# Expert blocks of 96 rows of one expert and 32 of the same or of a guest expert, in place of whole and half blocks; shared expert added to the residual before the routed experts

## The reference, cut to what matters

```python
T, D_MODEL, N_EXPERTS, MOE_TOPK, EXPERT_FF = 512, 1024, 64, 8, 256

def swiglu(h, wg, wu, wd):
    return (jax.nn.silu(h @ wg) * (h @ wu)) @ wd

def moe_ffn(h, ...):
    ...                                  # top_e, gw: 8 experts of each token and their weights
    # the tokens of each expert are laid out in blocks of 128 rows, padded
    def step(y, blk):
        tok, wt, e = blk
        out = swiglu(hf[tok], exp_gate[e], exp_up[e], exp_down[e])
        return y.at[tok].add(out.astype(F32) * wt[:, None]), None
    y, _ = lax.scan(step, jnp.zeros((T, D), F32), ...)
    shared = swiglu(hf, sh_gate, sh_up, sh_down)
    return (y.astype(h.dtype) + shared).reshape(B, S, D)

x = x + g2 * moe_ffn(h2, ...)
x = rms_norm_2(x, final_g)
```

## Time and profile before

| | us |
|---|---|
| median of 3 runs (2342.84 to 2349.06) | 2344.48 |
| span of the profiled execution | 2343.3 |
| first gate/up product of the experts starts | 1681.69 |
| last down product ends (2261.55 + 3.65) | 2265.20 |
| blocks stored | 51 (17 trips of 3) |

### The profile page before, as it was taken

One profiled execution on the slowest core, in us unless ns is written; L12 is line 12 of the kernel. 1 busy time (PEld: TensorE's weight loads), 2 busy tenths in 40 slices (PEclk: granted clock), 3 DMA queues, 4 the chain that ended last, 5 costly groups with the idle time before them and its releaser, 6 DMA issues. The chain is left out here.

```text
span 2343.3 us, 27600 instructions
## 1 busy us (share of the span) xinstructions
PE 2151.4 (92%) x10395; PEld 1246.3 (53%) x10395; DVE 1330.6 (57%) x2524; ACT 461.2 (20%) x916; POOL 396.7 (17%) x771
## 2 busy tenths in 40 slices
PE   6999989999999999999879999998699999999975
PEld 3444554777785458883443788445333333333322
DVE  3448863766672134434968333535766766767745
ACT  2013561121120011004235232011011111111111
POOL 0005000111000000000000000000444444444433
PEclk9999999999999999999989999998799999999988
DMA  9422000535524015981111100401499999898976
GB/s 389 180 81 81 36 1 20 233 144 216 215 81 179 36 72 229 391 306 54 37 57 58 51 3 4 177 36 54 180 372 397 425 353 421 344 407 357 413 281 252
DMA packets 68999, 446.60 MB, mean 191 GB/s; under 512 B 12276, under 2 KB 12932, under 8 KB 44066
## 3 DMA queue, kind: packets, MB, share of 16 engines
q0 software_dynamic: 36176, 254.42, 27.1%
q1 hardware_dynamic: 32722, 190.78, 21.0%
HBM read 416.27 MB, written 73.45 MB: 209 GB/s over the span
## 5 line engine op out<-in xcount | busy, mean ns | idle before, releaser
L965 PE MATMUL psum<-arena 128*128 128x256 f32 x1904 | 416.7, 381 | 2.1 <-PEq L1005 2.0
L2824 PE MATMUL psum<-arena 128*64 128x512 f32 (+1 forms) x1088 | 366.1, 600 | 38.9 <-DVE arena L2872 16.6
L965 PEld LDWEIGHTS psum<-arena 128*128 128x128 f32 x1904 | 361.4, 190 | 62.6 <-issue 14.0
L2872 DVE STREAM_TRANSPOSE arena<-arena 32x256 f32<-32x256 f32 x832 | 362.1, 435 | 15.8 <-DMA arena<-scratch_h,arena 4.1
L2824 PEld LDWEIGHTS psum<-arena 128*64 128x64 f32 (+1 forms) x1088 | 143.8, 165 | 226.6 <-issue 197.7
L2815 PE MATMUL psum<-arena 128*64 128x512 f32 (+1 forms) x544 | 186.2, 598 | 1.2 <-ACT arena L2850 1.2
L1067 PE MATMUL psum<-arena 128*128 128x512 f32 x352 | 151.8, 592 | 0.3 <-PEq L1091 0.3
L2815 PEld LDWEIGHTS psum<-arena 128*64 128x64 f32 (+1 forms) x544 | 68.5, 163 | 113.2 <-issue 111.8
L869 PE MATMUL psum<-arena 128*128 128x512 f32 x256 | 111.2, 593 | 2.3 <-DVE arena L2432 1.5
L1067 PEld LDWEIGHTS psum<-arena 128*128 128x128 f32 x352 | 66.6, 190 | 83.4 <-issue 83.4
L2878 DVE COPY arena<-psum 128x512 f32<-128x512 f32 x51 | 35.3, 692 | 132.7 <-PE psum L2815 132.7
(11 more groups left out here) (521 smaller groups left out, 2932.0 us busy)
## 6 DMA issues: line engine op xcount, KB each, us to landing
scratch_expert_out<-arena SPq DMA_DIRECT2D x18, 2048.0 KB, 19.9
scratch_expert_out<-arena SPq DMA_DIRECT2D x51, 512.0 KB, 9.9
arena<-in_w_ada SPq DMA_DIRECT2D x12, 2048.0 KB, 16.8
arena<-in_ada_w POOLq DMA_DIRECT2D x12, 2048.0 KB, 8.8
arena<-in_w_up SPq DMA_DIRECT2D x22, 1024.0 KB, 4.8
arena<-in_w_in SPq DMA_DIRECT2D x9, 2048.0 KB, 11.0
arena<-in_w_down SPq DMA_DIRECT2D x5, 2048.0 KB, 8.6
arena<-in_w_o SPq DMA_DIRECT2D x2, 2048.0 KB, 8.4
```

Of the source, the lines that this page charges most:

```text
L965: last = pe.matmul(out, w[:, k, :], x[:, k, :], start=(k == 0), stop=(k == KH - 1))
L2824: last = pe.matmul(K.bank[2 + s][r, :], xt[:, s, P * k + r.start:P * k + r.stop], gu[:, lane, 2 * E_FF * k:2 * E_FF * (k + 1)], start=(k = ...
L2872: last = dve.transpose(channels[c:c + 32, :, a:a + 32], tokens[a:a + 32, :, c:c + 32])
```

## The change

Blocks of 128 rows stay, and so do three lanes a trip. Each block has now a host expert on rows 32 to 127 and, on rows 0 to 31, either the host again or a guest expert. A host's part of more than 96 tokens takes all 128 rows; experts of up to 32 tokens are one guest piece, experts of 33 to 64 tokens two guest pieces or, where pieces are too many, a host of their own. `phase_route` plans this: it counts hosts, spare guest places and pieces, and spreads the pieces over the places, with two more small matmul groups on PE for their order. Each lane has two sets of weights, host and guest (`OWN`, `VISITOR`), each skipped by an index out of bounds where it is there already. PE reads for each block from the table which of the two the first 32 rows use (`choice`), and issues three matmuls in place of one: rows 32 to 63, rows 64 to 127, rows 0 to 31 (`rows_of`). Both loads of a lane share one semaphore, so a product waits for both.

To make room, the shared expert no longer stays: POOL multiplies its down weights by the gate `g2` and adds its output to the residual in `phase_route`; `phase_combine` starts its sum with a multiplication. Some buffers are shared: the third gathered block lies in a buffer that the routing used, so POOL waits for DVE once before it clears it; `h` is written in place of `g`; `ht` has one buffer.

The core of the diff:

```diff
-LANES, LANE = 4, 32
+LANE = 32
+GUEST = 32
+STATIC = BLOCK - GUEST
 ...
+            pe.wait_ge(spare_done.sem, 1)
+            order_mm.by(pe.matmul(K.bank[0][:, 0:1], const[:, RC_BEFORE:RC_BEFORE + P], num[:, 15:16], start=True, stop=True))
             gate_up(3)
+            free(K, gu_mm)
             pe.wait_ge(eb_done.sem, 1)
-            eb_t.by(pe.matmul(K.bank[3][:, 0:P], K.ones[:, :], diag[:, :], start=True, stop=True))
-            free(K, gu_mm)
-
-            w = take(K, pe)[:, 0:2 * D].rearrange("p (k n) -> p k n", k=2)
+            eb_t.by(pe.matmul(K.bank[3][:, P:2 * P], K.ones[:, :], diag[:, :], start=True, stop=True))
+            pe.wait_ge(guests_done.sem, 1)
+            pe.matmul(K.bank[3][:, 2 * P:2 * P + EXPERTS], visit[:, :], match[:, :], start=True, stop=True)
+            pe.matmul(K.bank[3][:, 2 * P + EXPERTS:3 * P], visit[:, :], match2[:, :], start=True, stop=True)
+            guests_mm.by(pe.matmul(K.bank[3][:, 3 * P:4 * P], K.ones[:, :], diag2[:, :], start=True, stop=True))
+
+            take(K, pe)
+            w = shared_down
+            pe.wait_ge(gated.sem, 2)
 ...
+            pool.wait_ge(K.ws_landed[down_at % 2].sem, 16 * (down_at // 2 + 1))
+            pool.wait_ge(gate_in.sem, 16)
+            for k in range(2):
+                gated.by(pool.tensor_tensor(shared_down[:, k, :], shared_down[:, k, :], gate_row[:, :], ALU.mult))
+            for t in range(NT):
+                pool.wait_ge(sh_out.sem, 2 * t + 2)
+                added.by(pool.tensor_tensor(K.res[:, t, :], K.res[:, t, :], shared[:, t, :], ALU.add))
 ...
+            step(stt(out=few[:, :], in0=cnt, scalar=GUEST + 0.5, in1=parts[:, :], op0=ALU.is_lt, op1=ALU.mult))
+            step(stt(out=many[:, :], in0=cnt, scalar=2 * GUEST + 0.5, in1=parts[:, :], op0=ALU.is_lt, op1=ALU.mult))
+            step(tt(host[:, :], parts[:, :], many[:, :], ALU.subtract))
+            step(tt(many[:, :], many[:, :], few[:, :], ALU.subtract))
 ...
+            link(dve, dve.tensor_reduce(FREE, got2[:, :], AX.X, ALU.add), spare_done)
 ...
+            step(dve.tensor_copy(visit[:, :], V.to_broadcast([P, P])))
+            step(tt(pieces[:, :], guest[:, :], second[:, :], ALU.add))
+            scan(piece_end, pieces)
 ...
+            dve.wait_ge(order_mm.sem, 1)
+            step(dve.tensor_copy(TURN, K.bank[0][:, 0:1]))
+            step(ts(TURN1, TURN, 1.0, None, ALU.add))
+            for to, place_, who in ((match, want, guest), (match2, later, second)):
+                step(ts(to[:, :], place_[:, :], TURN, None, ALU.is_ge))
+                step(stt(out=to[:, :], in0=place_[:, :], scalar=TURN1, in1=to[:, :], op0=ALU.is_lt, op1=ALU.mult))
+                step(stt(out=to[:, :], in0=who[:, :], scalar=FREE, in1=to[:, :], op0=ALU.mult, op1=ALU.mult))
 ...
+    gu, down = [], []
+    for lane in range(U):
+        gu.append(sb(f"e_gu{lane}", [P, 2, KD * 2 * E_FF]))
+        down.append(sb(f"e_down{lane}", [P, 2, 2 * D]))
+    xt, out = sb("e_xt", [P, U, D]), sb("e_out", [P, U, D])
+    g, ht, xg2 = sb("e_g", [P, U, E_FF]), sb("e_ht", [P, E_FF]), sb("e_x", [P, 2, D])
+    xg = [xg2[:, 0, :], xg2[:, 1, :], K.weigh[:, :]]
+    rows, wrows = sb("e_rows", [P, 8]).bitcast(U32), sb("e_weight_rows", [P, 4 * U]).bitcast(U32)
 ...
+            def choice(i, s):
+                return pe.value_load(table[0:1, at(i, s)], min_val=OWN, max_val=VISITOR)
+
+            def rows_of(bank, left, weights, lane_pick, col, first, last_):
+                for r in (slice(GUEST, 2 * GUEST), slice(2 * GUEST, P)):
+                    pe.matmul(bank[r, :], left[:, r], weights[:, OWN, col:col + 512], start=first, stop=last_)
+                picked = weights[:, bass.ds(lane_pick, 1), col:col + 512].rearrange("p a n -> p (a n)")
+                return pe.matmul(bank[0:GUEST, :], left[:, 0:GUEST], picked, start=first, stop=last_)
+
+            def down_products(i, s, pick):
 
                 b = (s - 1) % U
                 blocks_done(pe, ht_out, i, s, -1)
-                landed(pe, down_in, i, s, -1)
+                landed(pe, down_in, i, s, -1, 32)
                 blocks_done(pe, out_act, i, s, -2)
                 blocks_done(pe, out_dve, i, s, -2)
                 for half in range(2):
                     for k in range(2):
-                        for r, lane in halves(b):
-                            last = pe.matmul(K.bank[5 + half][r, :], ht[:, b, P * k + r.start:P * k + r.stop],
-                                             down[:, lane, D * k + 512 * half:D * k + 512 * half + 512], start=(k == 0), stop=(k == 1))
+                        last = rows_of(K.bank[5 + half], ht[:, P * k:P * k + P], down[b], pick, D * k + 512 * half, k == 0, k == 1)
                 last.then_inc(down_mm.sem, 1)
 
+            picks = {}
+
             def step(i, s):
+                if s == 0:
+                    if not (isinstance(i, int) and i == 0):
+                        picks[U - 1] = choice(i, -1)
+                    picks[0] = choice(i, 0)
                 blocks_done(pe, turned, i, s, 0)
-                landed(pe, gu_in, i, s, 0)
+                landed(pe, gu_in, i, s, 0, 32)
                 for k in range(KD):
-                    for r, lane in halves(s):
-                        last = pe.matmul(K.bank[2 + s][r, :], xt[:, s, P * k + r.start:P * k + r.stop],
-                                         gu[:, lane, 2 * E_FF * k:2 * E_FF * (k + 1)], start=(k == 0), stop=(k == KD - 1))
+                    last = rows_of(K.bank[2 + s], xt[:, s, P * k:P * k + P], gu[s], picks[s], 2 * E_FF * k, k == 0, k == KD - 1)
                 last.then_inc(gu_mm.sem, 1)
                 if not (isinstance(i, int) and i + s == 0):
-                    down_products(i, s)
+                    down_products(i, s, picks[(s - 1) % U])
+                if s < U - 1:
+                    picks[s + 1] = choice(i, s + 1)
                 blocks_done(pe, product, i, s, 0)
                 for k in range(2):
-                    last = pe.transpose(K.bank[7][:, P * k:P * k + P], h[:, s, P * k:P * k + P], K.ident[:, :])
+                    last = pe.transpose(K.bank[7][:, P * k:P * k + P], g[:, s, P * k:P * k + P], K.ident[:, :])
                 last.then_inc(h_turned.sem, 1)
 
-            steps(pe, step, lambda n: down_products(n, U))
+            steps(pe, step, lambda n: down_products(n, U, pe.value_load(table[0:1, bass.ds(n + LANE * (U - 1), 1)], min_val=OWN, max_val=VISITOR)))
 ...
+                for who in (OWN, VISITOR):
+                    pool.tensor_copy(wrows[:, index + 2 * s + who:index + 2 * s + who + 1], K.source[:, who, at(i, s)]).then_inc(ready.sem, 1)
+                pool.wait_ge(ready.sem, 2 * (U * i + s + 1) if isinstance(i, int) else i * (2 * U) + 2 * (s + 1))
                 pool.tensor_tensor(wait_for[:, 4:5], K.rstd[:, 0:1], K.rstd[:, 0:1], ALU.add)
-                for _, lane in halves(s):
-                    offset = bass.IndirectOffsetOnAxis(ap=wrows[:, index + lane:index + lane + 1], axis=0)
-                    pool.indirect_dma_start(to[:, lane, :], None, src, offset, bounds_check=EXPERTS * P - 1, oob_is_err=False).then_inc(landed_[lane].sem, 16)
+                for who in (OWN, VISITOR):
+                    offset = bass.IndirectOffsetOnAxis(ap=wrows[:, index + 2 * s + who:index + 2 * s + who + 1], axis=0)
+                    pool.indirect_dma_start(to[s][:, who, :], None, src, offset, bounds_check=EXPERTS * P - 1, oob_is_err=False).then_inc(landed_[s].sem, 16)
 ...
+                    if isinstance(i, int) and i == 0 and s == 1:
+                        pool.wait_ge(weigh_step.sem, 3 * NT)
+                        link(pool, pool.memset(xg[U - 1], 0.0), cleared)
 ...
-                    used.by(dve.scalar_tensor_tensor(out=s, in0=yg[:, n % RING, :], scalar=K.weight[:, t, j:j + 1], in1=s, op0=ALU.mult, op1=ALU.add))
+                        used.by(dve.scalar_tensor_tensor(out=s, in0=yg[:, n % RING, :], scalar=K.weight[:, t, j:j + 1], in1=s, op0=ALU.mult, op1=ALU.add))
+                    else:
+                        used.by(dve.tensor_scalar(s, yg[:, n % RING, :], K.weight[:, t, 0:1], None, ALU.mult))
 ...
```

## The result

The changed kernel takes 2841.31 us (median of 4 runs, 2839.84 to 2843.17), the kernel before 2344.94 beside it: 1.211 times as long, 95% interval 1.2093 to 1.2127. The forecast was 2798, range 2700 to 3000. The profiled execution took 2839.84 us, its span 2837.4, so the span to account for is 2837.4 - 2343.3 = 494.1 us longer.

The account below looks back on a forecast made before the run. PE was taken to bound the experts' stage, DMA just above. 2343.3 - 583.5 + 1016 for 42 blocks + 7 slow start + 3.5 first loads + 11 routing = 2797, as median 2798 us; range 2700 to 3000.

Parts of the forecast that it names:

- What bounds the kernel: Experts' stage before: PE sets a floor of 32.3 us a trip; four weight sets meet the DMA ceiling just above.
- the trips: Experts' stage: 42 hosts make 14 trips in place of 17; by the old floor 97 us less.
- Sizes wait for each other: PE's expert products: tiles of different size take turns even on disjoint array parts; a block takes 24.2 us, was 10.8.
- the first rival: Experts' stage: the three tiles overlap, a block stays 10.8 us and DMA decides; 2314 us, chance 0.08.
- The pairing of C with the next A: PE's expert products: rows 0 to 31 run beside the next step's rows 32 to 63; 25 phases a block.
- the rival of 2972: PE's expert products: the two 32-column tiles do not pair, 28.3 us a block, 176 us more; chance 0.07.
- The price of a change: PE's expert products: each switch of tile size costs 0.095 us, in a phase of 0.955 us, 25 phases a block.
- The upper bound of the same term, 0.16: PE's size switch costs at most an instruction's whole tail, 0.16 us: 25.8 us a block, +68 us.
- DMA, register reads, SP: Experts' stage: loads hide except +3.5 us at the first block; reads hide behind queued products; SP gets one more transfer.
- Routing: Routing stage: 42 more DVE steps take 12 us; shared down product and lists start later, +11 us (5 to 20).
- POOL's multiplications and additions, 2.4 us each, lie under the lists: Routing stage: GpSimd's new work for the shared expert, 2.4 us an instruction, is hidden and adds nothing.
- The end: Last stage: four DVE operations change their kind under PE's sum, costing 0.

Follow-up runs that it names:

- the sorted order: The changed kernel with each block's products sorted, all of the 64-row tile first, then those of the two 32-row tiles; 2686.46 us.
- four equal tiles: The changed kernel with the 64 fixed rows of every block multiplied as two tiles of 32 rows, so all tiles have one size; 2324.3 us.
- The split kernel before: The kernel before with lane 0's block as four tiles of 32 rows and lane 1's as 32, 64 and 32, one weight set each; 2586.85 us.

## Why the prediction was right, and what it mis-sized

**What bounds the kernel** and **the trips**: right. 478.3 of the 494.1 us are the experts' stage, with 42 blocks.

**Sizes wait for each other**: right, and no longer only for pairs of 64 and 128: the mixed block and the block of four in one execution show it for 32 beside 64. The section "Key Properties" of the Trainium skill's "TensorEngine Tiling (Array Packing)" (a change of the tiling mode drains TensorE) agrees with that. By "The mechanism" in the Trainium skill's "TensorE: Matmul & The Clock Gate" alone (different tile positions run at once) the changed kernel would have been the first rival, and the measurement, 25.16 us a block, decides against that reading for unequal tiles.

**The pairing of C with the next A**: right, it stands in the timeline; the rival of 2972 is out.

**The price of a change** is the term that was mis-sized: 0.095 us in the sum, 0.12 to 0.14 in the sorted order. The value came from two transposes and from two pairs of small products, and it is what the gap at a change measures, 0.09 us. The longer first wave after a change, 0.02 or 0.05 us, was not in it. One of the prediction's rows had it: the two transposes at 1798.81 come after the half-width down products of block 2, and take 0.27 us to the next group of their own size, where 0.215 was reckoned. 25 x 0.035 = 0.9 us is nearly all of the 0.97 by which a block is longer than forecast (25.16 against 24.19), and 42 x 0.97 = 41 us nearly all of the 43 us by which the forecast was low. The upper bound of the same term, 0.16, covered it.

**DMA, register reads, SP**: right. PE's only wait for `in_exp_gu` is the first, and the start grew by 3.7 us (forecast 3.5): the first product came 16.2 us after DVE's last instruction of the routing, which ended at 1665.5, and now comes 19.9 after 1685.6. The register reads would show with four equal tiles and no guests' loads, where they are still made: from the second distance on every block takes 10.81 us, the first of a trip too.

**Routing**: the count of DVE's steps was right: the shared products were to start some 10 us later by it, and start 10.0 later, counted from where the shared expert begins. The failed step is "POOL's multiplications and additions, 2.4 us each, lie under the lists". Only the additions do; they run at the same time as the lists, but each holds one DVE instruction until it ends, 7.4 us in all. With the 2.6 us from ahead of the shared expert the routing ends 20.1 us later, where 11 were forecast. The Trainium skill's "SBUF — State Buffer", section "Who interferes with whom", says that VectorE and GpSimd lock a shared pair of ports for a whole instruction, where VectorE has two inputs in SBUF or runs in a two-port mode. The rows agree for two inputs (2.52 us for a sum beside an addition or a multiplication) and for MAX8, which has one and is not held. The cast and the list steps have one tensor input as well and are held; whether they ran in a two-port mode no row here shows.

**The end**: forecast 0, measured -8.0. Most of it is not the change: in the profiled execution of before, DVE waited 7.39 us ahead of the second token tile's sum. The split kernel before has the same code there, no such wait, and 71.4 us from the last down product to the end, against 70.1 in after. The changed kind of operation gives some more: 0.75 us for the first of three where it was 1.28, on the path for all token tiles but the first, 1.6 us. What caused that wait of 7.39 us stays open.

**Added up**: +38.8 us in the experts' stage against the forecast's 1023, +9.3 up to the first product, -8.0 at the end: 40 us on the span. That the last two nearly cancel is luck: one is the additions and a difference of executions, the other for the most part a wait in before. The median of the runs stands 3.9 us above the profiled span, where it was 1.2.

## What to carry to other kernels

Cut a block into tiles of one size, even if that takes more multiplications: a step of four products of 32 columns took two waves of 0.43 us here, a step of 32, 64 and 32 took 1.99 us. If the sizes must differ, sort the products by size; every change was about 0.13 us, and a mix at every step paid it 25 times a block. Before work is put on GpSimd "beside" VectorE, look at VectorE's instructions in the stretch where it will run: sums of two inputs, a cast and list steps of 0.2 to 0.4 us lasted here as long as GpSimd's, one for each, while MAX8 did not. Where VectorE waited for TensorE afterwards, that cost nothing.

## What the runs showed of the hardware that was not expected

**A wait for weights costs a second time.** With four equal tiles, after 4.75 us without work the waves of PE come 0.85 us apart instead of 0.43, at the lower of the two clock levels (1.2 of 2.4 GHz), and go back to 0.43 after five of them. The timeline of PE, and a window over the slow waves, with a granted clock of 0.50:

```profile
1758.97 1.07 PE L2872 MATMUL psum<-arena 128*32 128x512 f32 x3 [4.75 <-DMA arena<-in_exp_gu,arena]
...
1759.80 1.10 PE L2872 MATMUL psum<-arena 128*32 128x512 f32 x3
...
1763.13 0.61 PE L2872 MATMUL psum<-arena 128*32 128x512 f32 x3
1763.56 0.61 PE L2872 MATMUL psum<-arena 128*32 128x512 f32 x3
```

```profile
1759.00:1762.50 3.50, 3.50 (x19) 1.44 (x23) 2.61 (x6) 0.00 (x0) 2.56 (x7) 0.50 0.99 415
```

PE's 15 waits for weights after the first product are 59.1 us, but the blocks' distances are 84 us longer than 41 x 10.81; of the other 25 us, 4 are a wait for DVE and 21 are these slow waves. Not every wait has them: after the two shortest, 0.93 and 1.59 us, the waves are 0.43 us apart. The forecast of the first rival had the bytes alone.
